# Whole modulation products moved from VectorE to GpSimd beside the branches, and one group choice for both halves

## The chip, the cores and the metric

One core of a Trainium2 chip runs the whole program: two layers of a transformer block (first block) and two layers of a second block, on 256 tokens of width 1024, in float32. The metric is the device time in microseconds of one execution. The profile gives engine times inside one execution: TensorE (PE, and PEld for its weight loads), VectorE (DVE), ScalarE (ACT), GpSimd (POOL) and SyncE (SP), which issues nearly all loads.

## The reference, cut to what matters

```python
for l in range(2):
    mod = c_act @ w_mod[l] + b_mod[l]          # 1024 -> 6 * 1024
    sh_m, sc_m, g_m, sh_f, sc_f, g_f = split(mod, 6)
    h = rms_norm(x, norm_mix_g[l]) * (1 + sc_m) + sh_m
    x = x + g_m * mixer(h)     # branches: differential attention, gated conv (31 taps), stick-breaking attention
    h = rms_norm(x, norm_ffn_g[l]) * (1 + sc_f) + sh_f
    x = x + g_f * moe_ffn(h)   # router: 8 groups of 8 experts, best 4 groups, then best 8 experts
```

In the router, scores are sigmoids of 64 logits; a group's score is the sum of its two best biased scores; the four best groups stay, and of their experts the eight best are chosen. The chosen scores are normalised and scaled.

## The kernel before, in words

Each engine has one program, written as Python generators that are run side by side while the program is built. A generator that yields an event's name goes on when that event is known, and PAUSE hands the turn to the next stream, so the order of instructions on an engine is written out by hand; at run time an engine takes its instructions strictly in that order. `K.ev[name]` is a semaphore with the value that stands for the event.

A layer goes: norm, projections, **branches**, **merge**, router and shared expert (`*_moe_start`), experts, sum. In the branches two streams of attention heads (`*_diff`), one of stick-breaking heads (`*_stick`), the conv and a fifth stream are stepped in turn by `side_by_side`. On TensorE the fifth stream is `pe_beside`: gate projections of 8 matmuls (L271, inside the helper `products`) that fill the time between the steps of the heads. The conv is 124 taps on VectorE (L1270, each 128x256; a fused multiply-add of two tensors in SBUF); 92 of them are issued in the projections, 32 in the branches, four at a time (`dve_conv_end`). A differential head on VectorE is: scores from PSUM plus mask (L1414), maximum (L1417), its negative (L1419), and after ScalarE's exponentials L1422, L1426, L1427, L1429, whose result `d_a` TensorE turns (L1355). A stick-breaking head is L1502, L1507, L1511; TensorE's L1454 needs L1507. L1550 and L1554 centre and scale the conv's sum for its norm.

The modulation vectors of this layer's second half and of the next layer are worked out as eight **items** per layer: one item is a 1024x512 piece of `w_mod` in the ring, as a tile of 128 partitions x 8 x 512. VectorE multiplies each of the eight 512-wide rows by a column of the conditioning vector (`K.cact`) and adds it to the row before: one tensor_scalar (L804) and seven scalar_tensor_tensor (L807), in place. TensorE then sums over the partitions with a matrix of ones (L820), ScalarE copies the row (L835), and GpSimd writes it to DRAM (L847) and, after each second item, reads the whole vector back as columns (L856). Items 0 to 3 belong to the branches on VectorE, and items 4 to 7 to the merge (`dve_merge`). TensorE's places for the sums are fixed: items 0, 1 and 2 between gate projections (`DIRECT_BESIDE`), item 3 behind the first output projection.

Loads go through one queue (SyncE, L551) in a fixed order, into a ring of eleven 1 MB units. A load waits until what lay in its units has been used by TensorE, an item's units by its L820. The order near the branches is: gate half, item 0, gate half, item 1, gate half, item 2, gate half, item 3, first output projection, item 4 and so on.

In the router VectorE works on both halves of the tokens (2 x 128) with small instructions: L1925 to L1930 for both, then L1938 to L1958 for each half in turn (the loop over `i`), then the weights (L1960 to L1972), the products of the shared expert (L1975) and the triangular matrix `K.below` (L1977), which also tells the event `chosen`. TensorE works meanwhile on the shared expert and on transposes of h (L1834), and counts the places (L271) once `chosen` is told.

Of the kernel before, what the change touches and what calls it, by code (L numbers as in the profile page):

```python
# [11 lines left out]
ALU = mybir.AluOpType  # L12
# [796 lines left out]
            yield PAUSE  # L809


def pe_direct(K, l, ns, only=None):

    te = K.te
    for item in direct_items(l, ns):
        w = direct_weights(K, item)
        b = yield from K.bank(("direct_row", *item), only=only)
        te.wait_ge(*(yield ("direct", *item, 7)))
        for t in range(4):
            ins = te.matmul(b[32 * t:32 * t + 32, 0:P], K.ones[:, 0:32], w[:, 7, t * P:(t + 1) * P], start=True, stop=True)  # L820
        ins.then_inc(*K.pe("direct_ps", *item, ps=b))
        K.pe.also("used", *item)
# [579 lines left out]
def dve_diff(K, l, heads):  # L1402
    ve, own, M = K.ve, K.dve.all, K.diff[heads[0]]
    s, st, a = M["s"], M["st"], M["a"]
    mask = C(K, "causal")
    for hd in heads:
        for i in range(2):
            w = (i + 1) * P
            yield PAUSE
            for mp in range(2):  # L1410
                ve.wait_ge(*(yield ("d_qk", l, hd, i, mp)))
                if mp == 0:
                    ve.wait_ge(*own())
                ve.scalar_tensor_tensor(s[:, mp, 0:w], K.ps["d_qk", l, hd, i, mp][:, 0:w], 0.125, mask[:, 256 - w:256],  # L1414
                                        ALU.mult, ALU.add).then_inc(*K.dve("d_s", l, hd, i, mp))
            ve.wait_ge(*own())
            ve.tensor_reduce(st[:, 0:2], s[:, :, 0:w], AX, ALU.max).then_inc(*K.dve())  # L1417
            ve.wait_ge(*own())
            ve.tensor_scalar(st[:, 2:4], st[:, 0:2], -1.0, None, ALU.mult).then_inc(*K.dve("d_neg", l, hd, i))  # L1419
            yield from pause(2)  # L1420
            ve.wait_ge(*(yield ("d_exp", l, hd, i, 1)))
            ve.reciprocal(st[:, 6:8], st[:, 4:6]).then_inc(*K.dve())  # L1422
            ve.wait_ge(*own())
            if i == 1 or hd != heads[0]:
                ve.wait_ge(*(yield ("d_turned", l, *((hd, 0) if i == 1 else (heads[0], 1)))))
            ve.tensor_scalar(a[:, 0:w], s[:, 0, 0:w], st[:, 6:7], None, ALU.mult).then_inc(*K.dve())  # L1426
            ve.tensor_tensor(st[:, 7:8], st[:, 7:8], K.neglam[l], ALU.mult).then_inc(*K.dve())  # L1427
            ve.wait_ge(*own())
            ve.scalar_tensor_tensor(a[:, 0:w], s[:, 1, 0:w], st[:, 7:8], a[:, 0:w], ALU.mult,  # L1429
                                    ALU.add).then_inc(*K.dve("d_a", l, hd, i))  # L1430
            yield from pause(3)
        yield from pause(4)
        ve.wait_ge(*(yield ("d_rstd", l, hd)))
        ve.scalar_tensor_tensor(K.oa[:, hd, :], K.ps["d_pv", l, hd][:, 0:256], K.sublnS[l], M["a"], ALU.mult,
                                ALU.mult).then_inc(*K.dve("d_oa", l, hd))
# [123 lines left out]
def side_by_side(first, second, stick, conv, later):  # L1559

    for f in (first, first, first, stick):
        yield from step(f)
    streams = [first, second, stick, conv, later]
    while streams:
        for f in list(streams):
            if not (yield from step(f)):
                streams.remove(f)
# [14 lines left out]


def dve_branches(K, l):
    yield from side_by_side(dve_diff(K, l, (0, 2)), dve_diff(K, l, (1, 3)), dve_stick(K, l), dve_conv_end(K, l),
                            dve_beside(K, l))


def dve_beside(K, l):

    yield from dve_direct(K, l, range(4))


DIRECT_BESIDE = {(0, 5): (0,), (1, 1): (1,), (1, 5): (2,)}
# [141 lines left out]

def pool_branches(K, l):
    yield from pool_mods(K, l, BEFORE_ROPE[l] + 1, len(early_parts(l)))
    yield from pool_direct(K, l, range(3))


def pool_merge(K, l):
# [173 lines left out]
def dve_moe_start(K, l):  # L1916
    ve, own = K.ve, K.dve.all
    dve_scale(K, K.affn[l], K.mods[l][:, 0, 4, :], K.gffn[l])
    ve.wait_ge(*own())
    yield from dve_norm(K, ("ffn", l), 256, 256, K.h, [K.affn[l]], K.r1)  # L1920
    sc, bi, mk, posm, rep = K.sc, K.bi, K.mk, K.posm, K.rep
    s8, gs, rank, cmp1, cmp2, top8, den = K.s8, K.gs8, K.rank, K.cmp1, K.cmp2, K.top8, K.den
    ve.wait_ge(*own())
    ve.wait_ge(*(yield ("scores", l)))
    ve.tensor_tensor(bi, sc, K.brow[l].unsqueeze(1).to_broadcast([P, 2, 64]), ALU.add).then_inc(*K.dve())  # L1925
    ve.wait_ge(*own())
    for q in range(16):
        ve.max(s8[:, q, :], bi[:, q // 8, (q % 8) * 8:(q % 8) * 8 + 8]).then_inc(*K.dve())
    ve.wait_ge(*own())
    ve.tensor_tensor(gs.rearrange("p i g -> p (i g)"), s8[:, :, 0], s8[:, :, 1], ALU.add).then_inc(*K.dve())  # L1930
    tri8 = C(K, "tri8").rearrange("p (a b) -> p a b", a=8)
    for i in range(2):
        ga = gs[:, i, :].unsqueeze(2).to_broadcast([P, 8, 8])
        gb = gs[:, i, :].unsqueeze(1).to_broadcast([P, 8, 8])
        bv = bi[:, i, :].rearrange("p (g e) -> p g e", g=8)
        mv = mk[:, i, :].rearrange("p (g e) -> p g e", g=8)
        ve.wait_ge(*own())
        ve.tensor_tensor(cmp1[:, i], gb, ga, ALU.is_gt).then_inc(*K.dve())  # L1938
        ve.tensor_tensor(cmp2[:, i], gb, ga, ALU.is_equal).then_inc(*K.dve())
        ve.wait_ge(*own())  # L1940
        ve.tensor_tensor(cmp2[:, i], cmp2[:, i], tri8, ALU.mult).then_inc(*K.dve())
        ve.wait_ge(*own())
        ve.tensor_tensor(cmp1[:, i], cmp1[:, i], cmp2[:, i], ALU.add).then_inc(*K.dve())
        ve.wait_ge(*own())
        ve.tensor_reduce(rank[:, i, :], cmp1[:, i], AX, ALU.add).then_inc(*K.dve())
        ve.wait_ge(*own())
        ve.tensor_scalar(gs[:, i, :], rank[:, i, :], 3.5, None, ALU.is_lt).then_inc(*K.dve())
        ve.wait_ge(*own())
        ve.tensor_tensor(mv, bv, ga, ALU.mult).then_inc(*K.dve())
        ve.tensor_scalar(rank[:, i, :], gs[:, i, :], 1.0, 1.0e30, ALU.subtract, ALU.mult).then_inc(*K.dve())  # L1950
        ve.wait_ge(*own())
        ve.tensor_tensor(mv, mv, rank[:, i, :].unsqueeze(2).to_broadcast([P, 8, 8]), ALU.add).then_inc(*K.dve())
        ve.wait_ge(*own())
        ve.max(top8[:, i, :], mk[:, i, :]).then_inc(*K.dve())
        ve.wait_ge(*own())
        ve.match_replace(rep[:, i, :], top8[:, i, :], mk[:, i, :], -3.0e38).then_inc(*K.dve())
        ve.wait_ge(*own())
        ve.tensor_tensor(rep[:, i, :], mk[:, i, :], rep[:, i, :], ALU.not_equal).then_inc(*K.dve())  # L1958
    ve.wait_ge(*own())
    ve.tensor_tensor(mk, rep, sc, ALU.mult).then_inc(*K.dve())  # L1960
    ve.wait_ge(*own())
    ve.tensor_reduce(den, mk, AX, ALU.add).then_inc(*K.dve())
    ve.wait_ge(*own())
    ve.tensor_scalar(den, den, 1e-20, None, ALU.add).then_inc(*K.dve())
    ve.wait_ge(*own())
    ve.reciprocal(den, den).then_inc(*K.dve())
    ve.wait_ge(*own())
    for i in range(2):
        ve.tensor_scalar(mk[:, i, :], mk[:, i, :], den[:, i:i + 1], 2.5, ALU.mult, ALU.mult).then_inc(*K.dve())
        ve.tensor_copy(K.tok_w[:, i, :, 0], C(K, "token")[:, i:i + 1].to_broadcast([P, 64])).then_inc(*K.dve())  # L1970
    ve.wait_ge(*own())
    ve.tensor_copy(K.tok_w[:, :, :, 1], mk).then_inc(*K.dve())  # L1972
    for j in range(2):
        ve.wait_ge(*(yield ("shared_silu", l, j)))
        ve.tensor_tensor(K.gs[:, j, :], K.ss[:, j, :], K.ps["shared_up", l, j][:, 256:512],  # L1975
                         ALU.mult).then_inc(*K.dve("shared_g", l, j))
    ve.tensor_tensor(K.below, K.ones, C(K, "from_s"), ALU.subtract).then_inc(*K.dve("chosen", l))  # L1977
    ve.wait_ge(*(yield ("ranks", l)))
    ps = K.ps["ranks", l]
    ve.scalar_tensor_tensor(posm, ps[:, 0:128].rearrange("p (i e) -> p i e", i=2), 1.0, rep, ALU.add,  # L1980
                            ALU.mult).then_inc(*K.dve())
    ve.wait_ge(*own())
    ve.tensor_scalar(posm, posm, -1.0, None, ALU.add).then_inc(*K.dve("places", l))
    ve.tensor_copy(K.count[0:64, :], ps[0:64, 128:129]).then_inc(*K.dve("count", l))
    ve.wait_ge(*own())
# [1818 lines left out]
```

## Time and profile before

| | |
|---|---|
| median of 3 runs | 2520.42 us (2520.07 to 2521.17) |
| the profiled execution's own time | 2525.26 us |
| its span in the trace | 2523.7 us |
| TensorE busy | 2444.7 us (97%) |
| VectorE busy | 812.8 us (32%), 2120 instructions |
| ScalarE busy | 511.4 us (20%) |
| GpSimd busy | 111.4 us (4%), 158 instructions |

The times in the trace count from the span's start. Layer 0's branches lie at about 162 to 262 us, layer 1's at about 1027 to 1126. A busy share is an average over stages; whether an engine holds up another is seen in the view of waits and in a stretch's timeline. Matmuls overlap their neighbours, so busy TensorE does not mean TensorE at its peak.

### The profile page before, as it was taken

How to read it: one execution, taken by the hardware profiler on the slowest of the kernel's cores; microseconds unless marked ns; L12 is line 12 of the kernel's file. 1: busy time of each engine (PE TensorE's matmuls, PEld its weight loads, DVE VectorE, ACT ScalarE, POOL GpSimd, SP SyncE). 2: the span in 40 equal slices, each digit the busy share in tenths (PEclk: the TensorE clock that was granted, in tenths of full speed). 3: DMA queues.
4: the chain of work that ended last, by engine and by line, in shares of the span. 5: the costliest groups of instructions: out<-in, count | busy, mean ns of one | idle time of the engine just before them, and what ended most of it. 6: DMA issues, size and time to landing. Idle time of an engine off the chain costs nothing. (4 is left out here: it accounts for less than half of the span.)

```text
span 2523.7 us, 30569 instructions
## 1 busy us (share of the span) xinstructions
PE 2444.7 (97%) x12107; PEld 1505.8 (60%) x12107; DVE 812.8 (32%) x2120; ACT 511.4 (20%) x1114; POOL 111.4 (4%) x158
## 2 busy tenths in 40 slices
PE   7999999999999899899999999999999999999998
PEld 4867885444444467688844444445446667664765
DVE  0596523121211116865322211111231322211154
ACT  2224211000000121341200000012221221211164
POOL 4000000000000001000000000000000000001110
PEclk9999999999999999999999999999999999999999
DMA  9644767999999998357599999998006111210310
GB/s 338 242 168 167 266 271 292 415 421 421 421 421 421 361 339 303 116 200 289 204 412 417 421 421 421 420 416 296 27 25 208 54 32 67 84 59 5 112 68 17
DMA packets 177434, 634.35 MB, mean 251 GB/s; under 512 B 13424, under 2 KB 47448, under 8 KB 127616
## 3 DMA queue, kind: packets, MB, share of 16 engines
q1 hardware_dynamic: 171296, 621.74, 63.1%
q0 software_dynamic: 5552, 10.52, 1.3%
q8 instruction: 100, 1.64, 0.3%
q14 instruction: 54, 0.44, 0.0%
q10 hardware_dynamic: 432, 0.01, 0.0%
HBM read 630.18 MB, written 3.42 MB: 251 GB/s over the span
## 5 line engine op out<-in xcount | busy, mean ns | idle before, releaser
L271 PE MATMUL ps<-hT,ring 128*128 128x256 f32 (+2 forms) x2480 | 645.4, 416 | 1.9 <-ACT ar L1491 1.9
L271 PEld LDWEIGHTS ps<-hT,ring 128*128 128x128 f32 (+1 forms) x2480 | 464.4, 190 | 171.2 <-issue 115.6
L2068 PE MATMUL ps<-ring,ar 128*32 128x512 f32 (+2 forms) x1328 | 331.9, 594 | 0.0
L2068 PE MATMUL ps<-ar 128*64 128x512 f32 (+2 forms) x720 | 275.7, 593 | 0.0
L2068 PEld LDWEIGHTS ps<-ring,ar 128*32 128x32 f32 (+2 forms) x1328 | 99.9, 124 | 197.1 <-issue 197.1
L2113 PE MATMUL ps<-ar 128*128 128x512 f32 x400 | 184.8, 604 | 0.0
L2042 PEld LDWEIGHTS ps<-ar,hT 128*128 128x128 f32 x1344 | 154.8, 192 | 12.0 <-issue 11.7
L2042 PE MATMUL ps<-ar,hT 128*128 128x128 f32 x1344 | 161.2, 276 | 0.0
L271 PE MATMUL ps<-ring,hT 128*128 128x256 f32 (+1 forms) x640 | 156.5, 402 | 0.0
L2384 DVE TENSOR_TENSOR ar<-ar,ps 128x256 f32<-128x256 f32 x50 | 21.1, 421 | 390.7 <-ACT ar L2233 384.5
L271 PEld LDWEIGHTS ps<-ring,hT 128*128 128x128 f32 x640 | 120.9, 190 | 40.1 <-issue 25.9
L271 PE MATMUL ps<-ring,ar 128*128 128x512 f32 x320 | 140.6, 596 | 0.0
L2113 PEld LDWEIGHTS ps<-ar 128*128 128x128 f32 x400 | 71.8, 188 | 111.6 <-issue 110.4
L2100 PE MATMUL ps<-ar 128*64 128x512 f32 (+1 forms) x272 | 131.3, 627 | 0.0
L2233 ACT ACTIVATE ar<-ps 128x256 f32<-128x256 f32 x50 | 19.2, 384 | 464.0 <-PE ps L2068 464.0
L271 PEld LDWEIGHTS ps<-ring,ar 128*128 128x128 f32 x320 | 60.8, 192 | 72.3 <-issue 70.9
L2100 PE MATMUL ps<-ring,ar 128*32 128x512 f32 (+2 forms) x256 | 96.7, 633 | 5.1 <-DMA ring<-in_w 3.7
L271 PE MATMUL ps<-ar,ring 128*128 128x256 f32 (+1 forms) x416 | 99.4, 396 | 0.6 <-ACT ar L1625 0.6
L2068 PEld LDWEIGHTS ps<-ar 128*64 128x64 f32 (+2 forms) x720 | 76.6, 124 | 37.3 <-issue 37.2
L1270 DVE SCALAR_TENSOR_TENSOR ar<-ar,wdw 128x256 f32<-128x256 f32 x240 | 98.1, 481 | 0.0
L2100 PE MATMUL ps<-xT,ar 128*64 128x512 f32 (+1 forms) x184 | 89.9, 635 | 0.0
L271 PEld LDWEIGHTS ps<-ar,ring 128*128 128x128 f32 x416 | 78.5, 190 | 18.4 <-issue 8.4
(452 smaller groups left out, 2633.5 us busy)
## 6 DMA issues: line engine op xcount, KB each, us to landing
ring<-in_w SPq DMA_DIRECT2D x198, 1024.0 KB, 18.3
ar<-in_w SPq DMA_DIRECT2D x124, 1024.0 KB, 15.5
ring<-in_w_mod SPq DMA_DIRECT2D x36, 2048.0 KB, 11.1
ring<-in_w_in SPq DMA_DIRECT2D x28, 2048.0 KB, 9.8
ring<-in_ab_w_in SPq DMA_DIRECT2D x28, 1024.0 KB, 11.9
xT<-in_w SPq DMA_DIRECT2D x23, 1024.0 KB, 19.1
cst<-in_w SPq DMA_DIRECT2D x21, 1024.0 KB, 22.6
hT<-in_w SPq DMA_DIRECT2D x18, 1024.0 KB, 21.9
```

The source lines that it names most:

```text
L271: ins = te.matmul(o, l, r, start=(first and i == 0), stop=(last and i == len(pairs) - 1), skip_group_check=lax)
L1270: ins = ve.scalar_tensor_tensor(K.acc[:, c, :], K.hpad[:, c, k:k + 256], tap, K.acc[:, c, :], ALU.mult, ALU.add)
L2042: ins = te.matmul(b[:, (k % 4) * P:(k % 4 + 1) * P], K.hx[:, i, k * P:(k + 1) * P], K.f_s[p % 2][:, i, :], start=(i == 0), stop=(i == 1))
L2068: ins = te.matmul(b[cols, :], K.x_b[:, kk, cols], weights_up(K, l, r)[:, :, kk, :], start=(kk == 0), stop=(kk == 7))
L2100: ins = te.matmul(b[cols, :], K.t_b[:, j * P + cols.start:j * P + cols.stop], weights_down(K, l, r, j, q), start=(j == 0), stop=(j == 1))
L2113: ins = te.matmul(K.banks[2 * i + q][:, :], K.wT[p % 2][:, i * P:(i + 1) * P], K.o_b[:, q * 512:(q + 1) * 512], start=False, stop=False, s ...
L2233: ac.activation(K.u_b, K.ps["up", l, p][:, 0:256], ACT.Silu).then_inc(*K.act("silu", l, p))
L2384: ve.tensor_tensor(K.g_b, K.u_b, K.ps["up", l, p][:, 256:512], ALU.mult).then_inc(*K.dve("g", l, p))
```

## The change

Two edits. The first takes items 0 to 3 off VectorE: GpSimd multiplies a whole item in one instruction (128 x 8 x 512, the conditioning vector broadcast along the last axis), and folds it with three additions, of the lower half onto the upper, of 4, 2 and 1 rows. It does items 0 and 1 ahead of any transfer of a sum, item 2 after row 0's transfer and item 3 after row 1's. VectorE's stream in the branches keeps only a place holder. TensorE waits for the last addition instead of VectorE's eighth piece. The second edit is in the router: the loop over the halves becomes one set of instructions over both (except the two searches for the eight largest and the two replacements), `K.below` is made at the start, and `chosen` is told as soon as the choice is there, ahead of the weights and the shared expert's products.

```diff
+def pool_direct_products(K, l, ns):
+    gp = K.gp
+    for item in direct_items(l, ns):
+        w = direct_weights(K, item)
+        gp.wait_ge(*(yield ("ring", *item)))
+        gp.tensor_tensor(w, w, K.cact[:, 0, :].unsqueeze(2).to_broadcast([P, 8, 512]),
+                         ALU.mult).then_inc(*K.pool("direct", *item, 8))
+        for n in (4, 2, 1):
+            gp.wait_ge(*K.ev["direct", *item, 2 * n])
+            gp.tensor_tensor(w[:, 8 - n:8, :], w[:, 8 - n:8, :], w[:, 8 - 2 * n:8 - n, :],
+                             ALU.add).then_inc(*K.pool("direct", *item, n))
...
+def direct_sum(l, item):
+    return ("direct", *item, 1 if item in direct_items(l, range(4)) else 7)
...
-        te.wait_ge(*(yield ("direct", *item, 7)))
+        te.wait_ge(*(yield direct_sum(l, item)))
...
 def dve_branches(K, l):
-    yield from side_by_side(dve_diff(K, l, (0, 2)), dve_diff(K, l, (1, 3)), dve_stick(K, l), dve_conv_end(K, l),
-                            dve_beside(K, l))
-
-def dve_beside(K, l):
-
-    yield from dve_direct(K, l, range(4))
+    yield from side_by_side(dve_diff(K, l, (0, 2)), dve_diff(K, l, (1, 3)), dve_stick(K, l), dve_conv_end(K, l), pause(1))
...
 def pool_branches(K, l):
     yield from pool_mods(K, l, BEFORE_ROPE[l] + 1, len(early_parts(l)))
-    yield from pool_direct(K, l, range(3))
+    yield from pool_direct_products(K, l, range(2))
+    for n in range(3):
+        yield from pool_direct(K, l, (n,))
+        yield from pool_direct_products(K, l, (2 + n,) if n < 2 else ())
...
 def dve_moe_start(K, l):
...
+    ve.tensor_tensor(K.below, K.ones, C(K, "from_s"), ALU.subtract).then_inc(*K.dve())
...
-    for i in range(2):
-        ga = gs[:, i, :].unsqueeze(2).to_broadcast([P, 8, 8])
-        gb = gs[:, i, :].unsqueeze(1).to_broadcast([P, 8, 8])
...
-        ve.tensor_tensor(cmp1[:, i], gb, ga, ALU.is_gt).then_inc(*K.dve())
...
+    groups = [P, 2, 8, 8]
+    ga = gs.unsqueeze(3).to_broadcast(groups)
+    gb = gs.unsqueeze(2).to_broadcast(groups)
...
+    ve.tensor_tensor(cmp1, gb, ga, ALU.is_gt).then_inc(*K.dve())
...
+    for i in range(2):
         ve.max(top8[:, i, :], mk[:, i, :]).then_inc(*K.dve())
-        ve.wait_ge(*own())
+    ve.wait_ge(*own())
+    for i in range(2):
         ve.match_replace(rep[:, i, :], top8[:, i, :], mk[:, i, :], -3.0e38).then_inc(*K.dve())
-        ve.wait_ge(*own())
-        ve.tensor_tensor(rep[:, i, :], mk[:, i, :], rep[:, i, :], ALU.not_equal).then_inc(*K.dve())
+    ve.wait_ge(*own())
+    ve.tensor_tensor(rep, mk, rep, ALU.not_equal).then_inc(*K.dve("chosen", l))
...
-    ve.tensor_tensor(K.below, K.ones, C(K, "from_s"), ALU.subtract).then_inc(*K.dve("chosen", l))
```

## Rows read from the trace of the kernel before

**Rows 1.** Table of stretches: length, busy us (instructions) of each engine, clock, DMA

```profile
core 0: us, PE busy (x) PEld busy (x) DVE busy (x) ACT busy (x) POOL busy (x), PEclk, DMA share, GB/s
162.00:200.00 38.00, 29.65 (x173) 23.18 (x166) 34.17 (x88) 15.61 (x43) 1.40 (x2) 0.97 0.62 221
200.00:262.00 62.00, 61.48 (x357) 51.18 (x357) 33.85 (x73) 25.41 (x70) 2.31 (x4) 0.96 0.48 170
...
412.00:870.00 458.00, 449.68 (x2690) 209.53 (x2687) 89.78 (x297) 38.87 (x74) 3.00 (x3) 0.99 0.99 411
...
1015.00:1064.00 49.00, 40.88 (x184) 28.24 (x183) 45.65 (x118) 15.93 (x44) 0.05 (x1) 0.97 0.38 130
```

**Rows 2.** TensorE's waits from 162 to 262 us: total, times, longest

```profile
PE ps L271 <- ACT xT L1625: 3.7, 1, 3.7
PE ps L1454 <- DVE ar L1507: 1.8, 1, 1.8
```

**Rows 3.** VectorE's timeline in the dense stretch: start, length, instruction, count

```profile
171.99 1.67 DVE L1270 SCALAR_TENSOR_TENSOR ar<-ar,wdw 128x256 f32<-128x256 f32 x4
...
199.01 0.75 DVE L807 SCALAR_TENSOR_TENSOR ring<-ring,par 128x512 f32<-128x512 f32 x1
```

**Rows 4.** GpSimd's timeline: start, length, instruction [idle before it <- releaser]

```profile
130.81 2.17 POOL L1332 TENSOR_TENSOR ar<-ar,cosT 128x512 f32<-128x512 f32 x1 [7.36 <-PE ps L1195]
139.75 1.59 POOL L1332 TENSOR_TENSOR ar<-ar,cosT 128x512 f32<-128x512 f32 x1 [6.77 <-PE ps L1195]
...
170.36 0.80 POOL L768 DMA_DIRECT2D ar<-mod_kept  x1 [4.92 <-DMA mod_kept<-ar]
210.56 0.60 POOL L847 DMA_DIRECT2D direct_kept<-ar  x1 [39.40 <-ACT ar L835]
...
240.28 0.57 POOL L856 DMA_DIRECT2D par<-direct_kept  x1 [6.05 <-DMA direct_kept<-ar]
...
1014.13 0.92 POOL L768 DMA_DIRECT2D ar<-mod_kept  x1 [4.44 <-DMA mod_kept<-ar]
```

**Rows 5.** GpSimd's groups by shape: count, busy us, mean ns, idle before

```profile
L3331 POOL TENSOR_TENSOR xT<-xT,ar 128x512 f32<-128x512 f32 x8 | 10.0, 1268 | 77.1 <-DVE ar L3294 77.1
L3429 POOL TENSOR_TENSOR ar<-ar,cst 128x256 f32<-128x256 f32 x10 | 7.4, 737 | 39.5 <-PE ps L3378 39.5
L3469 POOL TENSOR_SCALAR ar<-ar 128x256 f32<-128x256 f32 x8 | 6.8, 852 | 43.3 <-ACT ar L3459 43.3
...
L2863 POOL COPY hT<-xT 128x2048 f32<-128x2048 f32 x1 | 1.9, 1883 | 122.6 <-PE ps L2556 122.6
```

**Rows 6.** VectorE's taps beside GpSimd: two timeline rows; least/median/most ns at 139.5 to 142.3

```profile
128.20 3.65 DVE L1270 SCALAR_TENSOR_TENSOR ar<-ar,wdw 128x256 f32<-128x256 f32 x9
...
137.75 4.66 DVE L1270 SCALAR_TENSOR_TENSOR ar<-ar,wdw 128x256 f32<-128x256 f32 x9
...
L1270 DVE SCALAR_TENSOR_TENSOR ar<-ar,wdw x5: 471/476/1487, 139.3 to 141.9; 128x256 f32<-128x256 f32 x5
```

**Rows 7.** TensorE's timeline: turning of d_a, and item 3's sum

```profile
247.87 0.38 PE L1355 MATMUL ps<-cst,ar 128*128 128x128 f32 x2
...
277.61 0.43 PE L820 MATMUL ps<-ring,cst 128*32 128x128 f32 x8
```

**Rows 8.** Issue of item 3's load, and the w_mod loads' median us to landing

```profile
221.78 0.54 SPq L551 DMA_DIRECT2D ring<-in_w_mod  x1
...
ring<-in_w_mod SPq DMA_DIRECT2D x6, 2048.0 KB, 8.7
```

**Rows 9.** The router of layer 0: VectorE's and TensorE's timelines

```profile
383.40 0.22 DVE L1938 TENSOR_TENSOR ar<-ar 128x64 f32<-128x64 f32 x1
...
386.22 0.22 DVE L1938 TENSOR_TENSOR ar<-ar 128x64 f32<-128x64 f32 x1
...
395.20 0.29 DVE L1980 SCALAR_TENSOR_TENSOR ar<-ps,ar 128x128 f32<-128x128 f32 x1 [2.37 <-PE ps L271]
...
391.59 2.19 PE L1834 MATMUL ps<-cst,hT 128*128 128x128 f32 x16
```

More of the change, by code:

```diff
@@ L1930, in dve_moe_start @@
     ve.tensor_tensor(gs.rearrange("p i g -> p (i g)"), s8[:, :, 0], s8[:, :, 1], ALU.add).then_inc(*K.dve())
-    tri8 = C(K, "tri8").rearrange("p (a b) -> p a b", a=8)
-    for i in range(2):
-        ga = gs[:, i, :].unsqueeze(2).to_broadcast([P, 8, 8])
-        gb = gs[:, i, :].unsqueeze(1).to_broadcast([P, 8, 8])
-        bv = bi[:, i, :].rearrange("p (g e) -> p g e", g=8)
-        mv = mk[:, i, :].rearrange("p (g e) -> p g e", g=8)
-        ve.wait_ge(*own())
-        ve.tensor_tensor(cmp1[:, i], gb, ga, ALU.is_gt).then_inc(*K.dve())
-        ve.tensor_tensor(cmp2[:, i], gb, ga, ALU.is_equal).then_inc(*K.dve())
-        ve.wait_ge(*own())
[L1941 to L1953, printed above, removed]
@@ new lines, in dve_moe_start @@
+    groups = [P, 2, 8, 8]
+    tri8 = C(K, "tri8").rearrange("p (a b) -> p a b", a=8).unsqueeze(1).to_broadcast(groups)
+    ga = gs.unsqueeze(3).to_broadcast(groups)
+    gb = gs.unsqueeze(2).to_broadcast(groups)
+    bv = bi.rearrange("p i (g e) -> p i g e", g=8)
+    mv = mk.rearrange("p i (g e) -> p i g e", g=8)
+    ve.wait_ge(*own())
+    ve.tensor_tensor(cmp1, gb, ga, ALU.is_gt).then_inc(*K.dve())
+    ve.tensor_tensor(cmp2, gb, ga, ALU.is_equal).then_inc(*K.dve())
+    ve.wait_ge(*own())
@@ new lines, in dve_moe_start @@
+    ve.tensor_tensor(cmp2, cmp2, tri8, ALU.mult).then_inc(*K.dve())
+    ve.wait_ge(*own())
+    ve.tensor_tensor(cmp1, cmp1, cmp2, ALU.add).then_inc(*K.dve())
+    ve.wait_ge(*own())
+    ve.tensor_reduce(rank, cmp1, AX, ALU.add).then_inc(*K.dve())
+    ve.wait_ge(*own())
+    ve.tensor_scalar(gs, rank, 3.5, None, ALU.is_lt).then_inc(*K.dve())
+    ve.wait_ge(*own())
+    ve.tensor_tensor(mv, bv, ga, ALU.mult).then_inc(*K.dve())
+    ve.tensor_scalar(rank, gs, 1.0, 1.0e30, ALU.subtract, ALU.mult).then_inc(*K.dve())
@@ L1954, in dve_moe_start @@
+    ve.wait_ge(*own())
+    ve.tensor_tensor(mv, mv, rank.unsqueeze(3).to_broadcast(groups), ALU.add).then_inc(*K.dve())
+    ve.wait_ge(*own())
+    for i in range(2):
         ve.max(top8[:, i, :], mk[:, i, :]).then_inc(*K.dve())
-        ve.wait_ge(*own())
+    ve.wait_ge(*own())
+    for i in range(2):
         ve.match_replace(rep[:, i, :], top8[:, i, :], mk[:, i, :], -3.0e38).then_inc(*K.dve())
-        ve.wait_ge(*own())
-        ve.tensor_tensor(rep[:, i, :], mk[:, i, :], rep[:, i, :], ALU.not_equal).then_inc(*K.dve())
+    ve.wait_ge(*own())
```

## The prediction

> **What bounds the kernel now.** I first read the page's busy shares (TensorE 97%, VectorE 32%, GpSimd 4%), then the table of stretches. The reader is to see that TensorE has almost no idle time except where the three branches of a layer begin: of the 38 us from 162 to 200 it is busy for 29.65, and VectorE for 34.17; in layer 1 it is the same (40.88 of 49 us, VectorE 45.65). From 200 to 262 TensorE is full again (61.48 of 62) and VectorE half idle (33.85) [rows 1]. The view of waits says that in the first stretch TensorE waits for VectorE directly (L1507, 1.8 us) or through ScalarE's gate copies (3.7 us), which run behind VectorE's work [rows 2]. VectorE's timeline there is one dense chain: four conv taps (1.67 us, so 0.40 us apart), one piece of a modulation item (0.75 us), the next small step of a head, and so on without a gap until 199.8 [rows 3]. So in this stretch VectorE sets the pace; elsewhere in the branches TensorE does. What is late at the end of the branches is late at the end of the program: merge, router and experts follow on TensorE with hardly a hole (449.68 of 458 us in layer 0's experts, at a DMA share of 0.99), and the loads they need are released by TensorE's own progress, so they move with it [rows 1].
>
> **The change, part by part.**
>
> *VectorE is relieved.* Four items per layer, each 1 tensor_scalar and 7 fused multiply-adds of 128x512. Back to back a piece costs its start-to-start pitch, about 0.67 us (0.75 less the 0.08 by which neighbours overlap). Of the 32 pieces 10 stand in the dense stretch between 171.2 and 199.8 (counted in the timeline; its first and last rows are [rows 3]), so VectorE has some 7 us less to do there; the other 22 stand before or behind it, where TensorE is full or waits for nothing they hold up, and give nothing.
>
> *GpSimd is loaded.* Each item is now one multiplication of 128x4096 and additions of 128x2048, 128x1024 and 128x512. The rows have 0.737 us for 128x256 and 1.268 us for 128x512, so 2.07 ns an element and 0.2 us fixed [rows 5]: 8.7 + 4.4 + 2.3 + 1.3 = 16.7 us an item, 67 us a layer. Bounds of the multiplication, whose shape no row has: 3.7 us at the rate of the copy (1.88 us for 2048), 13.6 us at that of the tensor_scalar (0.85 us for 256) [rows 5]. It is a two-input tensor_tensor as L3331 is, so I take 8.7.
>
> *The two engines exclude each other.* This is the term that decides. At 139.75 GpSimd's L1332 began while VectorE ran conv taps; one tap, 0.476 us otherwise, took 1.487 us, and the nine taps 4.66 us, where the nine at 128.20 took 3.65 [rows 4, 6]. That is a stop of 1.01 us, as long as the GpSimd instruction still had to run. At 130.81 it was the other way round: GpSimd took 2.17 us instead of 1.27, so it got going at 131.71, as VectorE's nine taps ran out (128.20 + 3.65 = 131.85); it had waited 0.9 us [rows 4, 6]. Both have two inputs in SBUF. VectorE's steps that read one input from PSUM I take to run freely. The taps, L1427, L1429, L1507, L1550 and L1554 all have two inputs in SBUF.
>
> *Where this falls, layer 0.* GpSimd is free at 170.36 + 0.80 = 171.2 [rows 4]; item 0 has landed by then, item 1 before it is needed, and the two follow each other: 33.4 us of GpSimd instructions. VectorE has 28.6 us of work between 171.2 and 199.8, less 7 = 21.6, and some 16 of these are two-input steps (28 taps of about 0.4 us, four L1507, the small ones). In order, VectorE can do only what stands ahead of the next such step while GpSimd holds the port: about 4 us in all. So it reaches its point 199.8 at 171.2 + 33.4 + 21.6 - 4 = 222, some 22 us late, and TensorE with it, since it waited for VectorE there already. If VectorE is let in for whole runs of taps (as at 130.81) part of item 1's time slides into the stretch where VectorE has room; then 14 us. Between these I take 22.
>
> *Items 2 and 3.* GpSimd starts item 2 after it has sent row 0 (210.56 + 0.6 = 211.2 in times of before) and item 3 after row 1's column transfer (240.28 + 0.6 = 240.9) [rows 4]. Item 2's multiplication ends at 219.9, ahead of the next result that TensorE wants from VectorE in a two-input step, by several us: 1 us. Item 3's ends at 249.6, its first addition at 254.1, and TensorE turns d_a at 247.87 [rows 7]: 1.7 us late if VectorE gets through between the two, 6.2 us if not, and TensorE has no idle time to give. I take 4. Bounds for both together 0 and 10.
>
> *Layer 1.* GpSimd is free at 1014.13 + 0.92 = 1015.1 [rows 4], 20 us earlier against the branches (a row of before stands 864 us later), so item 0 falls on the conv taps that fill VectorE ahead of the branches. They are on the same chain: the same 33.4 us, the same 22 us.
>
> *Each layer* thus loses 22 + 1 + 4 = 27 us, two layers 54. At the bounds of the multiplication's price (5 us up or down an item, two items in the dense stretch) a layer loses 17 or 37.
>
> *A weighing of a page.* What the rows show is a stop under an instruction of 1.27 us; whether one of 8.7 us holds the port all through, they don't. The Trainium skill, page "SBUF — State Buffer", section "Who interferes with whom", says that a VectorE instruction with two SBUF inputs contends with a GpSimd one that reads SBUF, and that the one which comes first has the shared port pair for its whole instruction. By that rule 54 us stands; by the row taken narrowly (a stop of 1.01 us for each instruction) it is the mild case below.
>
> *PE's wait for the sums.* The load order and TensorE's places for the four sums stay. Item 0 is ready at about 188 and wanted at about 209, the fourth ready at 240.9 + 16.7 = 257.6 and wanted at 277.61 [rows 7]; its data, issued at 221.78 and 8.7 us under way, are there before 240.9 [rows 8]. What is queued behind the products on GpSimd are the row and column transfers of the items; row 2 goes out some 3 us later than before, and nobody needs its column before the merge's end.
>
> *The router.* The group choice of both halves in one set of instructions takes away most of one half's 2.82 us (383.40 to 386.22) and makes the first longer by about 0.06 us a step: 1.9 us less on VectorE a layer. "chosen" is also told before the weights and the shared products, nearly 6 us earlier. But TensorE is transposing from 391.59 for 2.19 us, and counts at 393.6, while VectorE had written the last thing needed at 395.20 - 2.37 = 392.8 and then waits 2.37 us for TensorE [rows 9]. So it is worth 0: TensorE's shared experts and transposes hide it. If that cover were gone it would give at most 1.9 us a layer.
>
> *The sum.* The median is 2520.42 us; the profiled execution took 2525.26 (span 2523.7), 0.2% more. The terms are differences, so they go on the median: 2520.4 + 54 - 0 = 2574 us.
>
> **The rivals.**
>
> *Mild contention, slower by little.* Each of 16 GpSimd instructions a layer stops VectorE once, by 1.0 us as at 139.75, or VectorE mostly keeps the port as at 130.81. Then 16 - 7 = 9 us a layer at most, 3 at least: 2526 to 2539. For it: the only two overlaps split evenly. Against: a stop lasted as long as the instruction did.
>
> *Faster.* VectorE loses the ten pieces and is hardly stopped (if, say, the broadcast multiplication leaves the port to the taps). It needs stops below 7 us a layer. The gain is bounded by TensorE's idle time there, 8.35 and 8.12 us [rows 1]; half of it is ordinary latency between engines. 2504 to 2515. Against it: [rows 6].
>
> *No change.* Relief and stops balance: 2516 to 2525.
>
> *TensorE also waits for the sums.* At the tensor_scalar's rate an item takes 25 us, and with VectorE let in between each pair the third or fourth sum comes after TensorE's place; some 10 us a layer on top: above 2596. Against: the 20 us of margin above.
>
> *The choice does more than I think:* 1.9 us a layer, 0.15%; it changes no case.
>
> **How the numbers follow.** Full contention 0.68 (its own range 2540 to 2596), mild 0.12, faster 0.12, no change 0.04, sums late too 0.04. The range for 8 in 10 takes the first two: 2526 to 2596. 0.2%, about what a measurement of this kernel can tell from no change, is 5 us. Faster 0.12, same 0.05, slower 0.83.
>
> **What would show it.** VectorE's taps beside GpSimd's products at several us instead of 0.48, and its whole time up although 64 instructions are gone; TensorE's idle time in the first 50 us of the branches up by some 20 us in each layer, released by VectorE or by ScalarE behind it; the sums ready before TensorE asks; the counting matmuls of the router starting as long after the router's logits as before, with VectorE waiting longer for them. The experts' stage as long as before. The prediction is wrong if the taps keep their 0.48 us, if GpSimd is stretched instead of VectorE, or if the multiplication is far from 8.7 us.

## The result and the profile after

The changed kernel takes 2587.88 us (2586.53 to 2588.72, 4 runs) against 2520.8 us: ratio 1.0254, 95% interval 1.0242 to 1.0266. It is slower by 67 us where 54 us were predicted. The profiled execution took 2587.79 us, its span is 2586.2, 62.5 us more than that of before, whose profiled execution was itself 4.8 us above its first median.

The table of stretches of the changed kernel, layer 0, with the same columns as [rows 1]; what stood at 171 to 200 us now lies at 172 to 222:

```profile
162.00:172.00 10.00, 10.00 (x72) 7.12 (x65) 7.15 (x22) 6.34 (x14) 1.31 (x2) 1.00 0.98 350
172.00:204.00 32.00, 6.03 (x27) 4.66 (x25) 31.97 (x11) 1.42 (x7) 31.26 (x9) 0.57 0.25 89
204.00:222.00 18.00, 15.70 (x74) 12.69 (x75) 16.55 (x48) 6.84 (x21) 0.00 (x0) 0.82 0.16 51
222.00:262.00 40.00, 35.85 (x207) 29.77 (x206) 22.50 (x36) 15.41 (x44) 17.30 (x6) 0.96 0.40 137
```

For 32 us GpSimd is busy (31.26), and VectorE seems to be (31.97), but with 11 instructions; TensorE runs for 6.03. Busy time is not work here: an instruction that waits for the port counts as busy. TensorE's granted clock, 1.00 while it worked, fell to the lower of its two levels (0.50, or 1.2 GHz) while it stood and stayed there from 180 to 210 us, through the first matmuls that came out of the waits; from 212 us on it was 1.00 again. Over the whole program TensorE's busy time is 2453.3 us, 8.6 more than before, for the same 12107 matmuls.

VectorE's timeline of the changed kernel in that stretch, to be held against [rows 3] and [rows 6]:

```profile
172.12 7.05 DVE L1437 TENSOR_SCALAR ar<-ar 128x2 f32<-128x2 f32 x1
179.08 8.99 DVE L1288 SCALAR_TENSOR_TENSOR ar<-ar,wdw 128x256 f32<-128x256 f32 x4
188.00 12.14 DVE L1525 SCALAR_TENSOR_TENSOR ar<-ar 128x384 f32<-128x384 f32 x2
200.06 4.76 DVE L1288 SCALAR_TENSOR_TENSOR ar<-ar,wdw 128x256 f32<-128x256 f32 x4
...
221.99 1.06 DVE L1525 SCALAR_TENSOR_TENSOR ar<-ar 128x384 f32<-128x384 f32 x2 [0.87 <-ACT ar L1502]
```

And GpSimd's timeline of the changed kernel, layer 0, beside [rows 4]:

```profile
171.29 0.80 POOL L768 DMA_DIRECT2D ar<-mod_kept  x1 [5.05 <-DMA mod_kept<-ar]
172.10 7.03 POOL L818 TENSOR_TENSOR ring<-ring,par 128x4096 f32<-128x4096 f32 x1
179.22 8.58 POOL L822 TENSOR_TENSOR ring<-ring 128x2048 f32<-128x2048 f32 x3
187.75 7.20 POOL L818 TENSOR_TENSOR ring<-ring,par 128x4096 f32<-128x4096 f32 x1
195.03 8.72 POOL L822 TENSOR_TENSOR ring<-ring 128x2048 f32<-128x2048 f32 x3
231.79 0.60 POOL L865 DMA_DIRECT2D direct_kept<-ar  x1 [28.04 <-ACT ar L853]
...
260.88 0.61 POOL L865 DMA_DIRECT2D direct_kept<-ar  x1 [12.14 <-ACT ar L853]
...
287.71 0.58 POOL L865 DMA_DIRECT2D direct_kept<-ar  x1 [4.81 <-ACT ar L853]
311.52 0.57 POOL L865 DMA_DIRECT2D direct_kept<-ar  x1 [23.23 <-ACT ar L853]
```

The reader is to see three things. The multiplication takes 7.03 us and an item some 15.7 (62.8 for the four), not 8.7 and 16.7. VectorE's L1437, two columns wide and 0.17 us long otherwise, took 7.05 us, as long as the multiplication under way; four taps took 8.99 beside the additions of item 0, and the two L1525 12.14 beside item 1. Less their usual lengths (0.17, 1.67, 1.06 and, for the next four taps, 1.67) VectorE's first four rows lost 28.4 of GpSimd's 31.6 us. And the four transfers of the sums stand at 231.79, 260.88, 287.71 and 311.52. Before they stood at 210.56, 233.65, 254.91 and 278.72 (the first and GpSimd's start are in [rows 4]). Less the 0.9 us by which GpSimd began later (171.29 against 170.36), the delay is 20.3, 26.3, 31.9 and 31.9 us. So items 0 and 1 cost 20.3 us, item 2 cost 6.0, item 3 cost 5.6, and the last transfer adds nothing. In layer 1 the same sums give 19.8, 6.7 and 5.8, in all 32.4.

TensorE's waits in the changed kernel, layer 0 from 160 to 300 us, then layer 1 from 1030 to 1190 us, where [rows 2] had 3.7 us at the top:

```profile
PE ps L1472 <- DVE ar L1525: 24.3, 2, 21.6
PE ps L1373 <- DVE ar L1447: 7.5, 2, 4.0
PE ps L1366 <- DVE ar L1452: 4.1, 1, 4.1
```

```profile
PE ps L1373 <- DVE ar L1447: 30.6, 3, 26.4
PE ps L1366 <- DVE ar L1452: 4.2, 1, 4.2
```

All of the new waiting is for VectorE, none for a sum of GpSimd. Of the 7.5 us for L1447 in layer 0, 3.5 lie in the dense stretch and 4.0 at item 3; the 4.1 us for L1452 lie at item 2. The router of layer 0 after the change, with its answers in [rows 9]:

```profile
416.55 0.29 DVE L1954 TENSOR_TENSOR ar<-ar 128x128 f32<-128x128 f32 x1
...
428.00 0.29 DVE L1997 SCALAR_TENSOR_TENSOR ar<-ps,ar 128x128 f32<-128x128 f32 x1 [2.57 <-PE ps L271]
...
424.39 2.19 PE L1849 MATMUL ps<-cst,hT 128*128 128x128 f32 x16
```

From the first comparison to the end of TensorE's transposes it was 391.59 + 2.19 - 383.40 = 10.4 us, now 424.39 + 2.19 - 416.55 = 10.0: TensorE goes its own pace, and VectorE still waits for its counts (2.57 us, 2.37 before).

### The profile page after: what moved, and what is told of

It reads as the page before. It is cut to its first block and busy times, and to the rows that moved or that the text cites. A ratio compares the mean times of both kernels' runs of the same rounds, so it can differ in the third digit from the quotient of the medians.

```text
span 2586.2 us, 30517 instructions
## 1 busy us (share of the span) xinstructions
PE 2453.3 (95%) x12107; PEld 1511.9 (58%) x12107; DVE 864.1 (33%) x2036; ACT 512.0 (20%) x1114; POOL 235.0 (9%) x190
## 5 line engine op out<-in xcount | busy, mean ns | idle before, releaser
L271 PE MATMUL ps<-hT,ring 128*128 128x256 f32 (+2 forms) x2480 | 654.1, 420 | 1.9 <-ACT ar L1509 1.9
L271 PEld LDWEIGHTS ps<-hT,ring 128*128 128x128 f32 (+1 forms) x2480 | 470.7, 193 | 173.9 <-issue 116.4
L1288 DVE SCALAR_TENSOR_TENSOR ar<-ar,wdw 128x256 f32<-128x256 f32 x240 | 139.3, 654 | 0.0
## 6 DMA issues: line engine op xcount, KB each, us to landing
xT<-in_w SPq DMA_DIRECT2D x23, 1024.0 KB, 19.4
```

Of the source, the lines that this page charges most:

```text
L271: ins = te.matmul(o, l, r, start=(first and i == 0), stop=(last and i == len(pairs) - 1), skip_group_check=lax)
L1288: ins = ve.scalar_tensor_tensor(K.acc[:, c, :], K.hpad[:, c, k:k + 256], tap, K.acc[:, c, :], ALU.mult, ALU.add)
```

## The experiments

**The two edits apart, and the relief alone.** router_only takes the kernel before with the second edit. no_products takes the changed kernel and leaves GpSimd's work on the items out, so that its sums are of raw rows:

```diff
 def pool_direct_products(K, l, ns):
-    for item in direct_items(l, ns):
...
+    yield from ()
 def direct_sum(l, item):
+    return ("ring", *item) if item in direct_items(l, range(4)) else ("direct", *item, 7)
```

> The kernel before with the router's edit alone; GpSimd and the items as before. My theory: TensorE's shared experts and transposes hide VectorE's choice, so VectorE works about 1.9 us less a layer and the time is that of before within 0.1% (2519 to 2523 us). Rival: the choice lies on the chain, 1.9 to 5 us a layer less, 2511 to 2517 us.

> The changed kernel with GpSimd's products and additions left out: TensorE sums the last raw row of items 0 to 3 as soon as the load has landed, so the modulation's values differ. VectorE is relieved, nobody holds the port. My theory, that the whole loss is the port: the time falls below that of before by what TensorE idles in the dense stretch, 4 to 8 us a layer, 2505 to 2513 us. Rival, that the loss has to do with the order of instructions, the load order or the later row transfers: well above 2530 us.

router_only: 2517.61 us against 2523.27, ratio 0.998 (0.9971 to 0.9989). That is outside what my theory allowed, though small; it is followed up below. no_products: 2506.88 us, ratio 0.9934 (0.9919 to 0.9949). So with neither engine doing the work and all else as in the changed kernel, the time is below before: order, loads and transfers cost nothing, and the whole loss comes with GpSimd's instructions. Against router_only the relief is worth some 11 us for both layers. The stretches of no_products that answer to the first two of [rows 1]:

```profile
162.00:200.00 38.00, 34.89 (x204) 26.57 (x204) 30.73 (x83) 16.98 (x46) 1.39 (x2) 1.00 0.63 222
200.00:262.00 62.00, 61.48 (x367) 51.64 (x366) 22.27 (x60) 28.76 (x78) 2.30 (x4) 1.00 0.53 184
```

TensorE is busy for 34.89 instead of 29.65 us of the 38, within the bound that the prediction's "faster" rival gave. There is a second part that neither the prediction nor that rival counts. Before, TensorE's last wait of the stretch (3.7 us) was followed by the lower clock level, 0.50 from 198 to 204 us; in no_products the clock is 1.00 throughout. What that level costs here is seen below at about 3 us a layer.

**Short pieces.** row_by_row cuts each GpSimd instruction into pieces of 128x512:

```diff
-        gp.tensor_tensor(w, w, K.cact[:, 0, :].unsqueeze(2).to_broadcast([P, 8, 512]), ALU.mult)
+        for k in range(8):
+            gp.tensor_tensor(w[:, k, :], w[:, k, :], K.cact[:, 0, k:k + 1].to_broadcast([P, 512]), ALU.mult)
```

and the additions likewise.

> The changed kernel with each of GpSimd's four instructions of an item cut into pieces of 128x512 (8 multiplications, 7 additions). The port is held for about the same time in all, some 16 us an item, but never for more than some 1.2 us at a stretch. Theory of the sum (what VectorE loses is the time GpSimd holds the port while VectorE has two-input work): 2580 to 2600 us, as the changed kernel. Theory of the long piece (what hurts is that one instruction holds the port for 7 us): the mild case, 2530 to 2550 us.

2568.85 us, ratio 1.0181 (1.0165 to 1.0196): between the two, 11 us below the lower end of the sum's range and 19 above the long piece's upper end. Both are partly wrong. GpSimd's groups of row_by_row from 160 to 300 us, and VectorE's timeline:

```profile
L826 POOL TENSOR_TENSOR ring<-ring 128x512 f32<-128x512 f32 x28 | 38.7, 1405 | 0.9
L820 POOL TENSOR_TENSOR ring<-ring,par 128x512 f32<-128x512 f32 x32 | 33.0, 1064 | 0.1
```

```profile
172.83 8.05 DVE L1440 TENSOR_SCALAR ar<-ar 128x2 f32<-128x2 f32 x1
180.79 4.69 DVE L1291 SCALAR_TENSOR_TENSOR ar<-ar,wdw 128x256 f32<-128x256 f32 x4
...
188.48 5.25 DVE L1291 SCALAR_TENSOR_TENSOR ar<-ar,wdw 128x256 f32<-128x256 f32 x4
...
196.70 5.02 DVE L1291 SCALAR_TENSOR_TENSOR ar<-ar,wdw 128x256 f32<-128x256 f32 x4
```

GpSimd's timeline of the same stretch:

```profile
172.83 8.02 POOL L820 TENSOR_TENSOR ring<-ring,par 128x512 f32<-128x512 f32 x8
180.93 10.17 POOL L826 TENSOR_TENSOR ring<-ring 128x512 f32<-128x512 f32 x7
191.06 8.97 POOL L820 TENSOR_TENSOR ring<-ring,par 128x512 f32<-128x512 f32 x8
```

The additions take turns with VectorE: taps at about 1.2 us each instead of 0.40, and 1405 ns an addition, GpSimd's own waiting in it. The first 8 multiplications did not let VectorE in: they held one step for 8.05 us, and the first eight of layer 1 held one tap for 8.83. But item 1's 8 multiplications, which have no more waits between them than the first, took turns with VectorE too: up to 1.22 us each, with taps of 1.25 beside them, here and in layer 1. What decides which of the two happens no run shows; in both layers turns began after GpSimd's first pause (0.08 us, before its first addition).

The four transfers tell where row_by_row saves against the changed kernel (12.2 us between the profiled spans; its profiled execution was 6.8 us above its median). In layer 0 items 0 and 1 cost 19.4 us (20.3 in the changed kernel), item 2 cost 3.8 (6.0) and item 3 cost 3.0, of which the last transfer gave back 0.9 (5.6). In layer 1 it is 19.8, 3.9 and 2.8 (19.8, 6.7 and 5.8). So where VectorE has two-input work all the time, cutting saves nothing, as the sum has it: GpSimd's total is even larger (71.7 us against 62.8 in the same window). Where VectorE comes only now and then, it saves about half, as the long piece has it.

**One pair at a time.** late_two puts items 0 and 1 back on VectorE (its edit follows), early_two items 2 and 3, which VectorE begins 16 rounds later:

```diff
-    yield from pool_direct_products(K, l, range(2))
...
-    return ("direct", *item, 1 if item in direct_items(l, range(4)) else 7)
+    return ("direct", *item, 1 if item in direct_items(l, (2, 3)) else 7)
...
-    yield from side_by_side(..., dve_conv_end(K, l), pause(1))
+    yield from side_by_side(..., dve_conv_end(K, l), dve_direct(K, l, range(2)))
```

> The changed kernel with items 0 and 1 back on VectorE and only items 2 and 3 on GpSimd. The port is then held only where VectorE has room in its time. From the changed kernel's trace items 2 and 3 cost 6.0 and 5.6 us of layer 0, so about 12 us a layer against before: 2540 to 2548 us. If only the dense stretch matters, as I had it in the prediction (5 us a layer): 2525 to 2533 us.

> Items 0 and 1 on GpSimd, items 2 and 3 on VectorE, the complement of late_two (which took 1.1% more than before). If what GpSimd costs adds up by item, this one takes the rest: after is 64 to 67 us above before, late_two 28 us, so some 38 us, 2555 to 2565 us. If the two pairs share one loss (the dense stretch's delay also gives the late items their place), the sum of both is more than the whole: 2570 to 2580 us.

late_two: 2551.45 us, 1.0108 (1.0092 to 1.0123), above both expectations. early_two: 2564.07 us, 1.0159 (1.0142 to 1.0176), 41 us above before, inside its first range. Its transfers put items 0 and 1 at 20.5 and 20.2 us in the two layers, as in the changed kernel. Together the two cost 28 + 41 = 69 us against 67, although the 6 us by which router_only is faster are counted twice in them; without those they are 34 and 47, 81 against 73. The surplus is late_two's own: by its transfers item 2 costs 9.5 us in layer 0, not 6.0. Its VectorE timeline shows why:

```profile
209.81 7.63 DVE L807 SCALAR_TENSOR_TENSOR ring<-ring,par 128x512 f32<-128x512 f32 x1
...
218.52 3.31 DVE L1437 TENSOR_SCALAR ar<-ar 128x2 f32<-128x2 f32 x1
```

VectorE runs into the multiplication of item 2 (begun at 209.84) at once, with a piece of item 1, which TensorE sums only at 240.80, and everything behind that piece waits too. In the changed kernel the same multiplication met VectorE after 4.5 us, at L1437. A stretch in which an engine has room by its busy share has no room for a stop of 7 us.

**Less time on the port.** folds_on_dve leaves the multiplication on GpSimd and does the three additions on VectorE:

```diff
+def dve_folds(K, l, ns):
+    for item in direct_items(l, ns):
...
+        for n in (4, 2, 1):
+            ve.wait_ge(*(yield ("direct", *item, 2 * n)))
+            ve.tensor_tensor(w[:, 8 - n:8, :], w[:, 8 - n:8, :], w[:, 8 - 2 * n:8 - n, :], ALU.add)
```

> The changed kernel with GpSimd doing the four multiplications (7.03 us each) and VectorE the three additions of each item (some 2.2, 1.1 and 0.6 us). GpSimd holds the port for 7 instead of 15.6 us an item, VectorE has about 4 us more of its own work an item. Theory of the sum: a layer loses 4 x 8.6 = 34 us less to the port and up to 16 us more to its own work, most of which lies where VectorE has room: 2530 to 2555 us. Theory of the long piece: the 7 us pieces are the ones that hurt, and they are all still there: above 2565 us.

2554.16 us, ratio 1.0125 (1.0108 to 1.0141): 31.5 us above before where the changed kernel is 67 above, at the upper edge of the sum's range and 11 us below the long piece's. GpSimd holds the port for 7.1 instead of 15.7 us an item, 45%, and the loss is 47% of the changed kernel's. That the two shares are so close is partly luck, for VectorE does three more additions an item. The long instructions are all there:

```profile
L818 POOL TENSOR_TENSOR ring<-ring,par 128x4096 f32<-128x4096 f32 x4 | 28.4, 7115 | 0.1
```

By its transfers in layer 0, items 0 and 1 cost 10.6 us, item 2 nothing and item 3 5.3. So in this kernel item 2's multiplication alone costs nothing; its 6 us in the changed kernel needed the additions.

**Is 0.2% real, and whose is it?** First before against itself:

> The kernel before, unchanged, timed against itself. It tells what a difference of 0.2% is worth here: router_only came out 0.2% below before, with the single runs of before between 2519.0 and 2525.6 us. If such a difference arises by chance, this one shows one of 0.1% or more too; if it is within 0.1%, the router's 0.2% is real. Its profile says which part of the profiled execution's 4.8 us over the first median was chance.

2523.83 us against 2522.61, ratio 1.0002 (0.9994 to 1.0011). So router_only's 0.2% is real. I then laid the TensorE timelines side by side by the number of the matmul. The router's own stretch comes out at one of two lengths with either kernel: from the 1641st to the 1901st matmul 54.0 us in before and in the changed kernel, 52.4 in before_again, router_only and router_padded. Before was granted the lower clock (0.50) from 373 to 375 us there, before_again 1.00. The difference stands nearly 500 us later, between the last expert of layer 0 and layer 1's projections. The same stretch in before_again and then in router_only, TensorE and VectorE:

```profile
872.54 3.43 PE L2556 MATMUL ps<-cst,hT 128*128 128x128 f32 x16 [5.77 <-issue]
...
874.95 1.27 DVE L2566 SCALAR_TENSOR_TENSOR xT<-ps,par,xT 128x256 f32<-128x256 f32 x3 [11.07 <-PE ps L2556]
878.38 2.05 DVE L2566 SCALAR_TENSOR_TENSOR xT<-ps,par,xT 128x256 f32<-128x256 f32 x5 [2.16 <-issue]
```

```profile
870.13 3.65 PE L2558 MATMUL ps<-cst,hT 128*128 128x128 f32 x16 [4.16 <-ACT ar L1202]
...
872.53 3.23 DVE L2568 SCALAR_TENSOR_TENSOR xT<-ps,par,xT 128x256 f32<-128x256 f32 x8 [9.46 <-PE ps L2558]
```

In before_again VectorE stops for 2.16 us in the middle of eight equal instructions, with nothing to wait for; in router_only it doesn't. The first profile of before has the stop as well (3.71 us), ahead of the same fourth instruction. TensorE's 5.77 us are not part of it: before had 4.17 there, released by ScalarE, and router_only 4.16. What does follow from the stop is the clock: before_again was granted 0.50 from 880 to 884 us, router_only 1.00 from 876 on. Two kernels ask what the stop depends on. products_only has the first edit without the second; router_padded is router_only with ten idle copies on VectorE, behind the choice, in place of the ten instructions that the edit saves:

```diff
+    for _ in range(10):
+        ve.wait_ge(*own())
+        ve.tensor_copy(s8[:, 0, :], s8[:, 1, :]).then_inc(*K.dve())
     ve.wait_ge(*(yield ("ranks", l)))
```

> The products on GpSimd alone, the router as before. In every run with the router's edit the stretch from layer 0's last expert to the start of layer 1 took 38.4 to 39.9 us, in both profiles of before 43.3 and 44.7, though no instruction of the router stands there; TensorE is idle there for 5.8 us that no engine releases. If the router's edit as such saves this, products_only shows some 44 us in that stretch and the time is about 5 us above the changed kernel's, 2590 to 2596 us. If it hangs on how many instructions VectorE's program has ahead of that point (the products take 32 away in each layer too), it shows 39 us, and the time is the changed kernel's, 2584 to 2590 us.

> The router's edit alone, with ten small copies added on VectorE (128x8 each, in place of the ten instructions a layer that the edit takes away) behind the shared expert's products, where VectorE waits for TensorE's counts. The choice is told as early as in router_only. If router_only's 0.2% comes from the earlier choice: 2517 us again, ratio 0.998. If it comes from where VectorE's instructions fall in the program: the time of before, ratio 1.000, with 43 us or more from layer 0's last expert to layer 1.

router_padded: 2522.81 us, ratio 1.000 (0.9989 to 1.001); the gain is gone, and the stop is back, again ahead of the fourth instruction:

```profile
872.08 1.27 DVE L2571 SCALAR_TENSOR_TENSOR xT<-ps,par,xT 128x256 f32<-128x256 f32 x3 [9.24 <-PE ps L2561]
877.23 2.05 DVE L2571 SCALAR_TENSOR_TENSOR xT<-ps,par,xT 128x256 f32<-128x256 f32 x5 [3.88 <-issue]
```

products_only: 2586.89 us, ratio 1.0246 (1.0228 to 1.0264), the time of the changed kernel. From the 4551st to the 4701st matmul:

| kernel | us | VectorE instructions fewer than before, a layer |
|---|---|---|
| before / before_again | 43.3 / 44.7 | 0 |
| router_padded | 44.6 | 0 |
| router_only | 38.4 | 10 |
| products_only | 38.4 | 32 |
| changed kernel | 39.6 | 42 |
| the other six | 38.4 to 39.9 | 10 to 42 |

So the earlier choice is worth nothing, as predicted, and the 0.2% comes with the number of VectorE instructions ahead of that place: the router's ten or the 32 pieces taken away remove the stop, ten idle copies bring it back. In all three profiles that have the stop it stands ahead of the same instruction, the 801st of those that VectorE's busy time counts, which points at the place in VectorE's program. What the engine waits for there no run shows.

**A version that beats both.** VectorE keeps all items, but begins them behind the dense stretch, and the sums come later; the router's edit is in:

```diff
 def dve_beside(K, l):
-    yield from dve_direct(K, l, range(4))
+    yield from pause(8)
+    pieces = dve_direct(K, l, range(4))
+    while (yield from step(pieces)):
+        yield from step(pieces)
+        yield PAUSE
-DIRECT_BESIDE = {(0, 5): (0,), (1, 1): (1,), (1, 5): (2,)}
+DIRECT_BESIDE = {(0, 7): (0,), (1, 3): (1,), (1, 6): (2,)}
```

> All items on VectorE as before, with the router's edit, but the pieces begin eight rounds later, two in every second round, behind the dense stretch, and TensorE's places for the sums of items 0 to 2 lie two to four gate projections later. No port is shared. no_products shows what relief of the dense stretch alone is worth, 16 us with the router's edit. If VectorE's order is all that holds TensorE there: 2505 to 2513 us. If the later sums hold up the loads that wait for the items' units: no gain over router_only (2517.6 us) or a loss.

2508.54 us, ratio 0.9942 (0.9929 to 0.9955), 14 us below before and 79 below the changed kernel. Its stretches, beside [rows 1]:

```profile
162.00:200.00 38.00, 34.89 (x206) 26.82 (x206) 34.43 (x89) 16.98 (x46) 1.39 (x2) 1.00 0.63 222
200.00:262.00 62.00, 60.00 (x360) 50.13 (x359) 38.23 (x84) 27.38 (x75) 2.30 (x4) 1.00 0.49 177
```

In the dense stretch TensorE gets all that no_products gives it (34.89), and its clock stays at 1.00 behind it. In the stretch that follows it loses 1.5 us (60.00 against 61.48). About 6 of the 14 us are the stop at layer 1's start, the rest the new order.

## Why the prediction was right, point by point

*VectorE sets the pace in the dense stretch:* right. Relief alone (no_products) brings TensorE 5 us there, and a delay of VectorE passes to TensorE. What TensorE's waits cost in clock had no term in the prediction.

*The two engines exclude each other, for the whole of an instruction:* right, and now shown for long ones: 7.05 us for a step of 0.17. By the rule of the Trainium skill that was weighed there ("SBUF — State Buffer", "Who interferes with whom") the trace agrees; the narrow reading of the row, a stop of 1.01 us whatever the length, falls.

*Which steps are stopped:* this was too narrow. I counted two-input steps alone. L1437 and L1444 are tensor_scalars with one input in SBUF, and in the changed kernel L1437 took 7.05 and 2.57 us, L1444 4.35, where 0.17 and 0.29 are usual. That section of the Trainium skill's page lists tensor_scalar among the operations that can take the shared pair; the trace agrees. Steps with an input in PSUM (L1432, L1520) and the reduction (L1435) kept their times beside the multiplications of items 2 and 3 (0.49 us for two L1432, 0.42 for L1435, 1.02 for two L1520), as assumed.

*Items 0 and 1, 22 us a layer:* 20.3 and 19.8, and part of that nearness is luck. GpSimd's time was overpriced, 31.6 us for both items instead of 33.4. VectorE got 3.3 of those us for its own work (31.6 less the 28.4 lost) where I had 4, though not by the steps that I had in mind: L1437 stopped it at once, and it got in where one GpSimd instruction followed another. It ended the stretch 23 us late (221.99 + 1.06 = 223.05, where it was 199.1, less the 0.9), and TensorE with it. TensorE then made up for 3 us by something that the prediction doesn't have. Before, its work behind the stretch ran at the lower clock (0.50 from 198 to 204 us), after it had stood for 3.7 us for ScalarE's gate copy [rows 2]; in the changed kernel that wait was gone, and the same work ran at 1.00 (222 to 229 us). TensorE's timeline before, then in the changed kernel:

```profile
198.77 3.78 PE L271 MATMUL ps<-ar,cst 128*128 128x256 f32 x8 [3.68 <-ACT xT L1625]
...
207.19 0.59 PE L1368 MATMUL ps<-ar,cst 128*128 128x256 f32 x2
```

```profile
222.95 1.96 PE L271 MATMUL ps<-ar,cst 128*128 128x256 f32 x8
...
228.42 0.59 PE L1386 MATMUL ps<-ar,cst 128*128 128x256 f32 x2
```

From the first to the last it was 8.4 us, and is 5.5. In layer 1 the same thing happens, also for 2.9 us.

*Items 2 and 3, 1 and 4 us:* this is the term that was mis-sized. They cost 6.0 and 5.6 us in layer 0, 6.7 and 5.8 in layer 1. The step that failed for item 2 is that I asked only when its multiplication ends, not its additions, and that I had left L1437 and L1444 free to run. L1437 lost 2.4 us to the multiplication; then L1444 and L1447 of one head took 4.35 and 2.37 us one behind the other, each until an addition ended, and TensorE waited 4.1 us for L1452. That step reads PSUM and wasn't stopped itself, but it stands behind them in VectorE's order. VectorE's timeline of the changed kernel there:

```profile
235.93 0.49 DVE L1432 SCALAR_TENSOR_TENSOR ar<-ps,cst 128x128 f32<-128x128 f32 x2 [4.14 <-PE ps L1366]
236.45 0.42 DVE L1435 TENSOR_REDUCE ar<-ar 128x2 f32<-128x256 f32 x1
236.91 2.57 DVE L1437 TENSOR_SCALAR ar<-ar 128x2 f32<-128x2 f32 x1
...
240.72 4.35 DVE L1444 TENSOR_SCALAR ar<-ar 128x128 f32<-128x128 f32 x1
...
245.17 2.37 DVE L1447 SCALAR_TENSOR_TENSOR ar<-ar 128x128 f32<-128x128 f32 x1
247.46 0.47 DVE L1452 SCALAR_TENSOR_TENSOR ar<-ps,par,ar 128x256 f32<-128x256 f32 x1
```

GpSimd's multiplication of item 2 ran from 232.41 to 239.45 us, its additions until 248.74. For item 3 I took the middle of 1.7 and 6.2 us, and the upper case came: L1447 took 4.62 us, until the first addition ended, and TensorE waited 4.0 us for it.

*The sums are ready in time:* right, no wait of TensorE names GpSimd.

*The router is worth 0:* right for its mechanism (router_padded), 6 us off for a reason that the prediction could not name.

*The sum:* 54 us predicted. In the profiles the layers lose 31.9 and 32.4 us, 64 in all, less 3.7 at layer 1's start (43.3 against 39.6), and the spans differ by 62.5; the rest are differences of 1 to 3 us either way elsewhere. The medians differ by 67; the profiled execution of before was itself 4.8 us above its median.

*The rivals:* mild contention falls with the stops themselves (6.9 us of L1437's 7.05) and with folds_on_dve, whose loss goes with the time on the port; faster and no change fall with the result; no_products puts a number on the bound of "faster", 2507.

## What to carry to other kernels

Work on GpSimd is not free for VectorE because GpSimd is idle: count its time on two-input operations as time taken from VectorE, for two-input steps and for tensor_scalars in SBUF, and ask where VectorE sets the pace. A low busy share is no cover against a long instruction: what counts is how long the next result that somebody waits for can be held up. A wait of a few us on TensorE can cost as much again in clock behind it (3.7 us, and then 3). And before moving work to another engine, try to move it in time on its own: here that gave some 8 us (14 with the vanished stop) where the other engine cost 67.

## What the runs showed of the hardware that I had not expected

A GpSimd multiplication with a broadcast second input took 7.03 us for 4096 elements, 1.7 ns an element, against 2.07 in [rows 5], whose second input is a full tensor. Eight GpSimd multiplications with no wait between them held VectorE as one would (8.05 us for L1440 of row_by_row, 8.83 for a tap in layer 1), and eight others, issued in the same way behind additions with which VectorE was taking turns, let it in after each (layer 1 of the same run, 1.25 us a tap). An instruction that waits for the port is counted as busy: VectorE's busy time rose from 812.8 to 864.1 us with 84 instructions fewer. And ten VectorE instructions more or fewer decide over 5 to 6 us at a place nearly 500 us behind the first of them (38.4 us in router_only, 44.6 in router_padded).
